# First layer's experts: 64 token slots as two 32-column matmuls instead of one of 64 columns

## The reference, cut to what matters

```
def expert_choice_ffn(h, router, w_gate, w_up, w_down):
    bsz, t, d = h.shape
    cap = CAPACITY_FACTOR * t // N_EXPERTS
    aff = jax.nn.softmax((h @ router).astype(jnp.float32), axis=-1)
    gates, idx = lax.top_k(jnp.swapaxes(aff, 1, 2), cap)
    xs = jax.vmap(lambda hb, ib: hb[ib])(h, idx)
    a = jnp.einsum('becd,edf->becf', xs, w_gate)
    u = jnp.einsum('becd,edf->becf', xs, w_up)
    y = jnp.einsum('becf,efd->becd', jax.nn.silu(a) * u, w_down)
    ...
```

## Time and profile before

| | |
|---|---|
| median of 3 runs | 2689.71 us (2687.33 to 2689.71) |
| profiled execution, from its first to its last instruction (its span, the only time that the profile gives of it) | 2682.2 us |
| what lies around the span, taken against the median | 7.5 us |
| TensorE busy (matmuls) | 2509.8 us, 94% of the span |
| VectorE, ScalarE, GpSimd busy | 48%, 37%, 15% |
| DMA moved | 567.73 MB, mean 212 GB/s |

### The profile page before, as it was taken

One profiled execution on the slowest core, in us unless ns is written; L12 is line 12 of the kernel. 1 busy time (PEld: TensorE's weight loads), 2 busy tenths in 40 slices (PEclk: granted clock), 3 DMA queues, 4 the chain that ended last, 5 costly groups with the idle time before them and its releaser, 6 DMA issues.

```text
span 2682.2 us, 35485 instructions
## 1 busy us (share of the span) xinstructions
PE 2509.8 (94%) x13952; PEld 1528.6 (57%) x13952; DVE 1293.2 (48%) x2488; ACT 987.1 (37%) x1876; POOL 409.9 (15%) x280
## 2 busy tenths in 40 slices
PE   6998997899999999897969999998999998999998
PEld 4875565433333333685744334442767887788886
DVE  3596445334444444587452333334765654442342
ACT  5216552234444443526523222223343343322222
POOL 0222102001111101223100000001214311122221
PEclk9999999899999999998989999999999998999999
DMA  6216714689999998320039999998122011222221
GB/s 263 81 48 226 276 65 184 246 328 377 386 389 387 390 384 336 126 85 11 32 136 422 420 421 421 421 421 353 64 92 66 17 32 48 87 95 96 93 87 55
DMA packets 85469, 567.73 MB, mean 212 GB/s; under 512 B 11760, under 2 KB 12016, under 8 KB 20280
## 3 DMA queue, kind: packets, MB, share of 16 engines
q1 hardware_dynamic: 79944, 550.15, 52.3%
q0 software_dynamic: 3616, 11.80, 1.9%
q10 hardware_dynamic: 1744, 3.51, 0.4%
HBM read 550.74 MB, written 14.68 MB: 211 GB/s over the span
## 4 chain that ended last, share of the span: by engine, by line
PE 47%; DVE 3%; DMA 2%; ACT 1%; issue 1%; POOL 0%; DVEq 0%; ACTq 0%
PE PS L1119 11%; PE PS L1236 4%; PE PS L1234 4%; PE PS L1235 4%; PE PS L1248 3%; PE PS L1250 3%; PE PS L1249 3%; PE PS L1193 2%; PE PS L1224 2%; PE PS L859 1%; DMA RF<-in_w_down_dram 1%; PE PS L1364 1%; DMA RING<-in_w_gate_dram 1%; PE PS L1266 1%; PE PS L1369 1%; PE PS L1280 1%
## 5 line engine op out<-in xcount | busy, mean ns | idle before, releaser
L2853 POOL TENSOR_TENSOR WHL<-RING,WHL 128x1024 fp32r<-128x1024 f32 x65 | 176.0, 2708 | 869.0 <-ACT WHL L1496 861.7
L1234 PE MATMUL PS<-RR,WHL 128*128 128x512 f32 x512 | 206.1, 403 | 1.8 <-DVE RR L2585 1.8
L1496 ACT ACTIVATE WHL<-RING 128x1024 fp32r<-128x1024 f32 x131 | 136.3, 1046 | 191.2 <-PE PS L1250 119.4
L1236 PE MATMUL PS<-RR,WHL 128*128 128x512 f32 x512 | 203.5, 397 | 0.0
L1235 PE MATMUL PS<-RR,WHL 128*128 128x512 f32 x512 | 202.0, 395 | 0.0
L1119 PE MATMUL PS<-RING,RF 128*64 128x512 f32 x816 | 186.1, 599 | 1.0 <-issue 0.7
L1119 PE MATMUL PS<-WIDE,RF 128*64 128x512 f32 x792 | 182.0, 596 | 0.0
L2056 DVE TENSOR_TENSOR WHL<-RING,WHL 128x1024 fp32r<-128x1024 f32 x66 | 82.1, 1245 | 141.9 <-ACT WHL L1496 139.3
L1789 ACT ACTIVATE RF<-PS,MODS,MSC 128x128 f32<-128x128 f32 x192 | 73.1, 444 | 179.4 <-PE PS L1193 127.7
L1119 PE MATMUL PS<-RF 128*64 128x512 f32 x544 | 127.5, 596 | 0.5 <-DMA RF<-in_w_down_dram 0.5
L1119 PE MATMUL PS<-X,RF 128*64 128x512 f32 x528 | 124.0, 601 | 0.4 <-DMA X<-in_w_down_dram 0.4
(11 more groups left out here) (408 smaller groups left out, 5131.0 us busy)
## 6 DMA issues: line engine op xcount, KB each, us to landing
RING<-in_w_gate_dram SPq DMA_DIRECT2D x61, 1024.0 KB, 16.0
WIDE<-in_w_down_dram SPq DMA_DIRECT2D x52, 1024.0 KB, 11.8
RING<-in_ada_w_dram SPq DMA_DIRECT2D x44, 1024.0 KB, 5.9
RING<-in_w_up_dram SPq DMA_DIRECT2D x42, 1024.0 KB, 7.8
X<-in_w_gate_dram SPq DMA_DIRECT2D x38, 1024.0 KB
AR<-in_w_up_dram SPq DMA_DIRECT2D x37, 1024.0 KB, 9.2
RF<-in_w_down_dram SPq DMA_DIRECT2D x31, 1024.0 KB, 13.8
RING<-in_w_in_dram SPq DMA_DIRECT2D x30, 1024.0 KB, 5.6
```

The lines of the kernel that those rows point to most:

```text
L1234: e.matmul(o, h[:, j, :], HTH2[:, j, :], start=j == 0, stop=False)
L1236: ins = e.matmul(o, lo[:, j, :], HTH2[:, j, :], start=False, stop=j == 7)
L1496: e.activation(h, load_buffer(ld)[:, js, cs], ACT.Copy).then_inc(act, A(("hi", st["i"])))
L2853: e.tensor_tensor(lo, load_buffer(loads[st["load"]])[:, js, cs], h.bitcast(F32), ALU.subtract).then_inc(pool, G(("lo", st["i"])))
```

## The change

Where context rows are carried (the first layer), each 64-column matmul of `tokens` becomes two of 32 columns: slots 0 to 31 go to quarter r/32, slots 32 to 63 to the next one. Both stream the same weight block. The rows of PSUM that they write are those of before, and so are the sums in them. The second layer keeps 64 columns.

```
                 def tokens(a, xs, st, w, begin, end):
+                    wide = 32 if need_ctx else 64
                     for i in range(4):
                         j, r = st["k0"] + i, 64 * (i % 2)
-                        ins = e.matmul(a[r:r + 64, :], xs[:, j, 0:64], w[:, i, :], start=begin and i < 2, stop=end and i > 1)
+                        for c in range(0, 64, wide):
+                            ins = e.matmul(a[r + c:r + c + wide, :], xs[:, j, c:c + wide], w[:, i, :], start=begin and i < 2,
+                                           stop=end and i > 1)
                     return ins
```

## The result

| | before | changed |
|---|---|---|
| median of 4 runs | 2688.52 us (2684.27 to 2689.71) | 2672.52 us (2668.87 to 2678.12) |
| profiled span | 2682.2 us | 2676.3 us |

The ratio is 0.995, with a 95% interval from 0.9934 to 0.9965: 16 us faster in the medians, while the two profiled executions are only 5.9 us apart.

The account below looks back on a forecast made before the run. TensorE was taken as the bound from 565.6 us on. Span 2682.2 less 9.5 for 68 merges gave 2672.7, plus 7.5 from span to median gave 2680.2 us; the range for 8 in 10 was 2677 to 2688.

Parts of the forecast that it names:

- What bounds the kernel: First layer's experts: TensorE, not the DMA engines, sets the pace from 565.6 us on.
- Step 1: Token matmuls of the first layer: twice the records at 32 columns keep rounds of 0.43 us, cost 0.
- Step 2: Where token and context blocks touch: 68 of 73 merges each save 0.14 us, 9.5 us in all.
- Step 3 and 4: First-layer experts: banks freed by VectorE cost 0 (2 us if wrong); weight loads reach 390 GB/s without starving TensorE.
- Step 5: Behind the experts: the chain through ScalarE and VectorE moves with TensorE's end, so the gain is kept.
- A: First-layer experts: TensorE cannot be fed the doubled instructions; slower, about 2735 us at 60 ns a record; chance 0.13.
- B: First-layer experts: the DMA engines are the true bound, up to all 9.5 us given back, 2683 to 2690; chance 0.11.
- C: Block borders: the 0.14 us comes from switching target bank or stationary rows and stays, 2689.7 us; chance 0.03.
- the last term of the sum: Whole execution: the median of the runs lies 7.5 us above the profiled span, turning 2672.7 into 2680.2 us.

Follow-up runs that it names:

- fewer_tokens: Changed kernel with two of the eight 128-row blocks of each first-layer token product left out; stage 522.8 us against 559.4, ratio to before 0.9844.
- flip_32: Changed kernel with each first-layer flip's eight 128-column transposes made into 32 matmuls of 32 columns; stage 565.6 us, ratio to before 0.9961.
- the pair without turn: Kernel before and changed kernel, each with every product opening with context; stages 580.1 and 559.7 us, ratios to before 1.0049 and 0.9945.
- the later comparisons: Changed kernel unaltered, timed twice more against before; medians 2676.76 and 2673.26 us, ratio 0.9955 both times.
- wide_rows: Changed kernel, first-layer context-row transposes in picks made matmuls reading all 128 partitions, upper 64 meeting zeros; stage 560.9 us, ratio to before 0.9964.
- halves_apart: Changed kernel's 32-column token matmuls reordered: all four blocks for slots 0 to 31, then for 32 to 63; stage 560.3 us, ratio to before 0.9963.

## Why the prediction was wrong, point by point

- *What bounds the kernel* was right. TensorE paces the stage in both kernels, with no wait for weights; fewer_tokens shows that transfers hold it up only when the stage is some 37 us shorter.
- *Step 1*, token rounds at 0.43 us and nothing for the doubled records: right, 1.71 us for a load, in the second layer as well.
- *Step 2*, the merges, was right in kind and slightly short in size. I took 68 x 0.14 = 9.5 us, leaving out the five contacts before the wait at 565.59. The stage gave 10.5 us, 73 contacts at 0.143. From that wait's end on it was 495.35 before (1060.94 - 565.59) and 485.64 after (1048.33 - 562.69), 9.7 us; the other 0.8 us came ahead of the wait, which moved forward with TensorE. The words "I count those at nothing" were wrong. Around the picks the next neighbour changed too, from 64 columns to 32, where the part on the change says that nothing changes; with 128 columns in between, a change of width stays there in both kernels.
- *Step 3 and 4*: no wait of TensorE appears from 575 to 1030 us; the loads run at 390 GB/s. A pair issued at 712.11 lands 9.7 us later and is first used at 740.03. Right.
- *Step 5*: right. L886 starts 19.1 us behind the stage's end in the changed kernel and 19.0 before, so the gain is not given back there.
- *Rivals*: A is out, since the stage kept its rounds of 0.43 us with 4227 matmul and 4222 weight-load records in 462 us, 55 ns a record, and in flip_32 they passed at some 10 ns each for 1.32 us; B is out at this speed, C is out by the pair without turn.
- **The step that failed is the last term of the sum, "the median of the runs is 7.5 us above the profiled span", and the range that was set around it.** In the changed kernel the median lies 3.8 us below the profiled span (2672.52 against 2676.3). The time around the span of one execution is 1.8 us (2678.12 against 2676.3). The other 5.7 us were the distance between one execution of before with a high clock and the median. And the range from 2677 held the uncertainty of the mechanism, but not that of the time: executions of one kernel cover 14 us (2679.46 to 2693.7 before, 2667.31 to 2681.14 changed), because spells at 1.2 GHz come and go, nearly all of them outside the stage. The three runs shown, within 2.4 us, looked tighter than the kernel is, and their median, 2689.71, was 2.3 us above the mean of the 64 later ones. With 10.5 us for the mechanism the forecast would have been near 2679, and the later comparisons, 2676.76 and 2673.26, both lie below it and below the lower end that I had given. Half of those 14 us below 2679 would have put the lower end near 2672, just under the result.
- The forecast was thus 7.7 us too high. Of these, 2.3 are the base of three runs, 1.0 is the mechanism (10.5 in place of 9.5), 2.2 are the four runs of the changed kernel against the mean of its 17, and the 2 that are left are open. The mechanism's 10.5 us are shown in the profiles; the rest of the measured 16 is not a gain that was traced to the change.

## What to carry to other kernels

Where TensorE is the bound, read its timeline by start times and compare a block with its rounds: what is left is the price of changing the array's shape, about 0.14 us each time here, for columns and for rows, and it is won back by giving neighbours one shape, even at twice the instructions (64 columns as 2 x 32) or twice the tile, as long as the array time grows by less than the borders cost; in flip_32 and wide_rows it grew by more. Size such a gain in the stage by a profile of each kernel, since whole executions scatter by more than it. Before a range is set, ask how far executions of the kernel lie apart, and do not take the distance of a profiled span from the median as a constant.

## What the runs showed of the hardware that was not expected

- Work for four column quarters runs side by side although the program names them as 0, 2, 0, 2, 1, 3, 1, 3 (1.72 us a load in halves_apart, as in the interleaved order, and four records started within 0.05 us at a block's start).
- An f32 transpose by TensorE is one record, an f32 matmul against the identity two, and the same flip took 1.32 us as matmuls in place of 0.81.
- 64 matmul records and their weight loads, of which the trace holds 60, passed in 1.32 us on four quarters (flip_32).
- DMA shares of 1.00, 1.00 and 1.02 went with 382, 390 and 402 GB/s in one stage with the same transfers; only who waits for whom told which engine was the bound.
